# Sums of squares for six residual norms: GpSimd adds seven tiles, TensorE sums two

## The reference

```python
def rms_norm(x, g):
    xf = x.astype(jnp.float32)
    y = xf * lax.rsqrt(jnp.mean(xf * xf, -1, keepdims=True) + NORM_EPS)
    return (y * g.astype(jnp.float32)).astype(x.dtype)

for l in range(DEPTH):                     # first stack
    h = rms_norm(x, attn_norm_g[l])
    ...
    x = x + merged @ w_out[l]
    h2 = rms_norm(x, mlp_norm_g[l])
    x = x + jnp.square(jax.nn.relu(h2 @ mlp_up[l])) @ mlp_down[l]
return rms_norm(x, final_norm_g)
...
for layer in range(DEPTH):                 # second stack
    h = rmsnorm(x, norm_mix[layer]) * (1.0 + sc1) + sh1
    ...                                    # y: a gated delta rule with attention, or latent attention
    x = x + g1 * y
    h = rmsnorm(x, norm_ffn[layer]) * (1.0 + sc2) + sh2
    x = x + g2 * peer_ffn(h, ...)
return rmsnorm(x, final_norm)
```

## Time and profile before

| | |
|---|---|
| median of 3 runs | 3479.36 us (3476.62 to 3481.10) |
| the profiled execution | 3475.42 us |
| its span in the profile | 3473.6 us |
| PE busy | 3393.0 us (98%) |
| DVE busy | 2452.4 us (71%) |
| ACT busy | 1631.6 us (47%) |
| POOL busy | 323.6 us (9%) |
| DMA, mean | 163 GB/s |

### The profile page before, as it was taken

One profiled execution on the slowest core, in us unless ns is written; L12 is line 12 of the kernel. 1 busy time (PEld: TensorE's weight loads), 2 busy tenths in 40 slices (PEclk: granted clock), 3 DMA queues, 4 the chain that ended last, 5 costly groups with the idle time before them and its releaser, 6 DMA issues.

```text
span 3473.6 us, 69683 instructions
## 1 busy us (share of the span) xinstructions
PE 3393.0 (98%) x24714; PEld 3070.1 (88%) x24714; DVE 2452.4 (71%) x5105; ACT 1631.6 (47%) x3275; POOL 323.6 (9%) x438
## 2 busy tenths in 40 slices
PE   8999999999999999999999999999999999999998
PEld 7879899988888998889988888888889888888887
DVE  6734457665434866537998888888538998888887
ACT  5153355433423743235555555555445555555554
POOL 0212000020210000000370000000000550000000
PEclk9999999999999999989999999999999999999999
DMA  8633378864335976234337887777444258787875
GB/s 231 177 90 94 110 220 268 239 178 136 87 93 155 270 233 162 62 88 138 111 101 195 196 196 191 197 195 186 106 132 151 84 135 195 193 194 194 195 195 135
DMA packets 644022, 565.20 MB, mean 163 GB/s; under 512 B 62027, under 2 KB 589402, under 8 KB 643546
## 3 DMA queue, kind: packets, MB, share of 16 engines
q1 hardware_dynamic: 638564, 542.16, 59.1%
q0 software_dynamic: 4960, 19.93, 1.7%
q10 hardware_dynamic: 278, 0.08, 0.0%
HBM read 550.52 MB, written 9.44 MB: 161 GB/s over the span
## 4 chain that ended last, share of the span: by engine, by line
PE 88%; DVE 7%; ACT 2%; issue 1%; DMA 1%; SPq 0%; POOL 0%; DVEq 0%; ACTq 0%; POOLq 0%
PE bank L1461 15%; PE bank L878 15%; PE bank L856 14%; PE bank L1481 7%; PE bank L1475 7%; PE bank L1478 7%; PE bank L899 4%; PE bank L1411 3%; PE bank L1436 2%; PE bank L852 2%; DVE uT L3331 2%; PE bank L1390 1%; PE bank L1270 1%; PE bank L967 1%; PE bank L1421 1%
## 5 line engine op out<-in xcount | busy, mean ns | idle before, releaser
L1461 PE MATMUL bank<-t_high,u_parts 128*128 128x256 f32 x3072 | 424.8, 280 | 1.3 <-ACT u_parts L2200 1.3
L1461 PEld LDWEIGHTS bank<-t_high,u_parts 128*128 128x128 f32 x3072 | 403.2, 188 | 20.9 <-ACT u_parts L2200 3.0
L3370 DVE TENSOR_TENSOR v_low<-ring,v_high 128x512 fp32r<-128x512 f32 x512 | 337.0, 690 | 59.7 <-ACT v_high L2212 35.4
L1481 PE MATMUL bank<-v_low,w_high 128*128 128x512 f32 x1024 | 323.1, 397 | 0.0
L1475 PE MATMUL bank<-v_high,w_high 128*128 128x512 f32 x1024 | 318.8, 392 | 0.9 <-ACT v_high L2212 0.9
L2212 ACT ACTIVATE v_high<-ring 128x512 fp32r<-128x512 f32 x512 | 299.2, 620 | 38.3 <-PE bank L1481 38.2
L1478 PE MATMUL bank<-v_high,w_low 128*128 128x512 f32 x1024 | 316.1, 390 | 0.0
L2415 POOL TENSOR_SCALAR uT<-cst,selT 128x128 f32<-128x128 f32 x256 | 188.2, 744 | 1312.7 <-ACT selT L2137 1308.4
L2200 ACT ACTIVATE u_parts<-bank 128x512 fp32r<-128x512 f32 x384 | 219.9, 594 | 191.3 <-DVE bank L3342 188.3
L1764 ACT ACTIVATE arena<-bank 128x256 f32<-128x256 f32 (+1 forms) x270 | 103.8, 387 | 437.7 <-PE bank L856 242.2
L856 PE MATMUL bank<-hT,ring 128*128 128x256 f32 (+2 forms) x1232 | 277.6, 382 | 8.3 <-DVE hT L2640 6.1
(11 more groups left out here) (467 smaller groups left out, 6423.7 us busy)
## 6 DMA issues: line engine op xcount, KB each, us to landing
ring<-in_peer_v SPq DMA_DIRECT2D x256, 512.0 KB, 4.5
ring<-in_peer_u SPq DMA_DIRECT2D x768, 128.0 KB, 4.3
ring<-in_w_in SPq DMA_DIRECT2D x128, 512.0 KB, 4.1
ring<-in_mlp_up SPq DMA_DIRECT2D x64, 512.0 KB, 4.2
uT<-in_mod_w SPq DMA_DIRECT2D x64, 512.0 KB, 5.1
ring<-in_mlp_down SPq DMA_DIRECT2D x64, 512.0 KB, 4.4
ring<-in_peer_u SPq DMA_DIRECT2D x64, 512.0 KB, 3.8
arena<-in_mod_w POOLq DMA_DIRECT2D x32, 512.0 KB, 4.9
```

Of the source, the lines that this page charges most:

```text
L1461: ins = eng.matmul(PB[6 + b][:, 0:S], u_parts[:, part, k * P:k * P + P], moving[:, k, :], start=(n == 0), stop=(n == len(products) - 1))
L1481: ins = eng.matmul(PB[2 * tt + q][:, :], w_high[:, b, t], v_low[:, j % 4, d], start=False, stop=last)
L3370: tt_(v_low[:, j % 4, d], ring[:, 2 + j % 4, d], v_high[:, d].bitcast(F32), ALU.subtract).then_inc(sem("vL_ready"), 1)
```

## The change

GpSimd gets the sum over the tiles. With each square that ScalarE signals, `squares_added` adds the running sum in place: square[1] = square[0] + square[1], up to square[6], which then holds the sum of tiles 0 to 6, and signals sq_added after each add. Each add waits for the one before. In down of layer 1 there are two adds in each step, first in hT, then in square. TensorE waits for the sixth sq_added, multiplies ones with tile 6, waits for the eighth sq_ready, and multiplies ones with tile 7. Nothing of the square sums is left between the projection's tiles. The other square sums (the first norm, the latent norms, the raw columns of the second stack's layer 1, the final norm) stay as they are.

```diff
-            def square_pair(k):
-
-                if k == 0 and pe.reused("ss_read", 1):
...
+            def residual_sum(k):
+
+                if k < KD - 1:
+                    return
+                if pe.reused("ss_read", 1):
+                    eng.wait_ge(sem("ss_read"), pe.freed("ss_read", 1))
+                eng.wait_ge(sem("sq_added"), pe.next("sq_added", KD - 2))
+                eng.matmul(PB[4][:, 0:S], C("ones"), square[:, KD - 2, :], start=True, stop=False)
+                eng.wait_ge(sem("sq_ready"), pe.next("sq_ready", KD))
+                eng.matmul(PB[4][:, 0:S], C("ones"), square[:, KD - 1, :], start=False, stop=True).then_inc(sem("ss_ready"), 1)
+
+            def residual_pair(k):
...
+                eng.wait_ge(sem("sq_added"), pe.next("sq_added", KD - 2))
+                for bank, sq in ((4, square), (5, hT)):
+                    eng.matmul(PB[bank][:, 0:S], C("ones"), sq[:, KD - 2, :], start=True, stop=False)
+                eng.wait_ge(sem("sq_ready"), pe.next("sq_ready", KD))
+                for bank, sq in ((4, square), (5, hT)):
+                    ins = eng.matmul(PB[bank][:, 0:S], C("ones"), sq[:, KD - 1, :], start=False, stop=True)
+                ins.then_inc(sem("ss_ready"), 1)
...
+            def to_residual(one):
 
                 for m in range(KD):
                     one(m)
-                    if m >= 2:
-                        square_in(m - 2)
-                for m in range(KD - 2, last):
-                    square_in(m)
...
+                to_residual(down)
                 if l == 0:
-                    to_residual(down)
+                    residual_sum(KD - 1)
                 else:
-                    to_residual(down, square_pair, last=0)
-                    raw_tiles([("conv", j) for j in range(RAW)], raw_conv, S + 1, square_pair)
+                    raw_tiles([("conv", j) for j in range(RAW)], raw_conv, S + 1, residual_pair)
...
+            def squares_added(both=False):
+
+                for k in range(KD):
+                    eng.wait_ge(sem("sq_ready"), pool.next("sq_ready"))
+                    if 0 < k < KD - 1:
+                        if k > 1:
+                            eng.wait_ge(sem("sq_added"), pool.seen["sq_added"])
+                        if both:
+                            tt_(hT[:, k, :], hT[:, k - 1, :], hT[:, k, :], ALU.add)
+                        tt_(square[:, k, :], square[:, k - 1, :], square[:, k, :], ALU.add).then_inc(sem("sq_added"), 1)
+                        pool.next("sq_added")
...
                 for b in (0, 3):
                     gated(l, b)
+                squares_added()
+                squares_added(l == 1)
...
             for l in range(DEPTH):
+                if l == 1:
+                    pool.next("sq_ready", KD + 6)
+                squares_added()
                 gate_rows(l)
```

More of the change, by code:

```diff
@@ L929, in norm_sum @@
                     square_sum(square, k, KD, bank)
-            def square_pair(k):
-                if k == 0 and pe.reused("ss_read", 1):
+            def residual_sum(k):
+                if k < KD - 1:
+                    return
+                if pe.reused("ss_read", 1):
                     eng.wait_ge(sem("ss_read"), pe.freed("ss_read", 1))
-                eng.wait_ge(sem("sq_ready"), pe.next("sq_ready"))
-                eng.matmul(PB[4][:, 0:S], C("ones"), square[:, k, :], start=(k == 0), stop=(k == KD - 1))
-                ins = eng.matmul(PB[5][:, 0:S], C("ones"), hT[:, k, :], start=(k == 0), stop=(k == KD - 1))
-                if k == KD - 1:
-                    ins.then_inc(sem("ss_ready"), 1)
-            def to_residual(one, square_in=lambda k: square_sum(square, k, KD), last=KD):
+                eng.wait_ge(sem("sq_added"), pe.next("sq_added", KD - 2))
[3 more added lines that the diff above has]
+            def residual_pair(k):
+                if k < KD - 1:
+                    return
+                if pe.reused("ss_read", 1):
+                    eng.wait_ge(sem("ss_read"), pe.freed("ss_read", 1))
[7 more added lines that the diff above has]
+            def to_residual(one):
                 for m in range(KD):
                     one(m)
-                    if m >= 2:
-                        square_in(m - 2)
-                for m in range(KD - 2, last):
-                    square_in(m)
             raws = [0]
@@ L1670, in _ @@
                 eng.wait_ge(sem("gated_b"), pe.next("gated_b", KD))
-                to_residual(lambda m: stream(("wout", l, m), lambda i: merged[:, i, :]), last=0)
+                to_residual(lambda m: stream(("wout", l, m), lambda i: merged[:, i, :]))
                 norms[0] += 1
-                raw_tiles([("up", l, j) for j in range(RAW)], raw_up, S, lambda k: square_sum(square, k, KD))
+                raw_tiles([("up", l, j) for j in range(RAW)], raw_up, S, residual_sum)
                 for j in range(RAW, DFF // P):
@@ L1724, in mix @@
                         stream(("mix", l, m), lambda i: mix_t[:, i, :])
-                to_residual(mix, last=0)
+                to_residual(mix)
                 norms[0] += 1
-                raw_tiles([("pq", l, j) for j in range(RAW)], raw_pq, S + 1, lambda k: square_sum(square, k, KD))
+                raw_tiles([("pq", l, j) for j in range(RAW)], raw_pq, S + 1, residual_sum)
                 experts(l)
@@ L2416, in gate_rows @@
                     ins.then_inc(sem("pool_rows"), 1)
+            pool.next("sq_ready", KD)
             for l in range(DEPTH):
```

## The result

The changed kernel took 3458.94 us (median of 5 runs, 3454.16 to 3464.89), the kernel before 3477.91 us on the same chip (5 runs, 3473.92 to 3481.1): ratio 0.9946, 95% interval 0.9935 to 0.9957, 19.0 us less. One of the later executions of the kernel before took 12505.4 us at a mean granted clock of 0.407; it counts in no figure here.

A forecast was written before the change was run, and what follows sets the result against it. TensorE, busy 98% of the span, was taken to set the pace. Gains 4.90 + 1.55 + 3.81 + 3.44 = 13.70 us against the 3479.36 us median gave 3465.7 us (chance 0.50), range 3460 to 3474.

The forecast's parts named there:

- mix, both: Mix stages of both layers: 2.15 us ahead of tile 7's end plus 0.30 in the tail, twice: 4.90 us gain.
- down 0: Down, layer 0: 2.15 us gained, less 0.60 because the sum comes later in the tail: 1.55 us gain.
- down 1: Down, layer 1, with two sums: 4.30 us gained, less 0.49 in the tail: 3.81 us gain.
- wout, both: Wout, both layers: the mod_w transfer sets the tail, only four slots of 0.43 us count per layer: 3.44 us gain.
- Rival A: Residual stages: every removed slot comes off, tails hidden or adds shorter: 18.06 us gain, 3461.3 us; chance 0.10.
- What one product costs: TensorE, ones times a tile of squares: one slot of 0.43 us, 42 products removed.
- The add in the tail: GpSimd's last add, after square 6: 0.73 us, with 0.15 us before its start and 0.05 to PE's start.
- 0.59 behind VectorE: Mix tail: GpSimd's add, begun inside VectorE's residual operation, ends 0.59 us after it, the same as unblocked.
- Rival B: Tails cost more: adds of 1.53 us (gain 9.7), mod_w landing unmoved (10.3), or both (6.3, 3473.1 us); chance 0.22.
- Rival C: Behind the stages: the gain is given back at a join that PE doesn't clock, 3479.4 us; chance 0.12.
- Rival E: The change doesn't do what it says: PE's order still has eight products; chance 0.02.
- Rival D: Down stages: GpSimd's add holds VectorE back from weight_low, PE waits: 13.8 us slower, 3493 us; chance 0.04.

The follow-up runs named there:

- e10: The kernel before, unedited, measured against itself: 3475.29 us, ratio 1.0000.
- second and third comparison: The changed kernel, unedited, timed again twice beside the kernel before: 3462.34 us (ratio 0.9962), then 3459.53 us (ratio 0.9953).
- e5: Changed kernel, but in the down stages GpSimd adds only tiles 0 to 5 and TensorE does three products: 3460.85 us, ratio 0.9962 to before.
- e6: Changed kernel with the first mod_w transfer of each first-stack layer issued two ring loads sooner: 3461.95 us, ratio 0.9964 to before.
- e2: Changed kernel without GpSimd's adds, so the sums of tiles 0 to 5 are missing: 3459.21 us, ratio 0.9951 to before.
- e4: Changed kernel with one more GpSimd operation in front of the last add of every residual: 3466.87 us, ratio 0.9975 to before.
- e3: Kernel before with all its products, plus GpSimd's adds, their sums unused; TensorE waits for the last add: 3480.57 us, ratio 1.0016.

## Why the prediction missed

**The sum was right.** Term by term, in us of gain; measured is the first pair of profiles, with the wout terms at equal landing of the mod_w transfer:

| term | forecast | measured |
|---|---|---|
| mix, both | 4.90 | 2.29 + 2.30 = 4.59 |
| down 0 | 1.55 | 1.44 |
| down 1 | 3.81 | 3.86 |
| wout, both | 3.44 | 1.73 + 1.72 = 3.45 |
| sum | 13.70 | 13.34 |

For wout 0 the profiles differ by 1.80, of which 0.07 is the landing (5.45 against 5.38). For wout 1 I set after against e10, 29.76 less 28.04, since the transfer took 5.05 and 5.06 in these two. In the first profile of before it took 6.25. VectorE's first use of it there:

```profile
1109.29 0.58 SPq L2458 DMA_DIRECT2D uT<-in_mod_w  x1
...
1115.54 0.76 DVE L3019 TENSOR_SCALAR arena<-uT,cond 128x1024 f32<-128x1024 f32 x1 [2.10 <-DMA uT<-in_mod_w]
```

So the first pair shows 2.92 in this stage, 1.2 of it not from the change. On average over the profiles such landings add 0.8 to the sum (14.1), and the runs say 14.2 at equal clock and 14.7 in their medians. I can't tell 13.3 from 14.7 by runs that scatter by 3 us.

**The step that failed is the base, and with it the range's low end.** The prediction set its sum of 13.70 against the median of three runs, 3479.36, which gave 3465.7, and not against the profiled execution's 3475.42, which gave 3461.7. All 69 runs of the kernel before put it at 3475.7: the base was 3.7 too high. Then the range took "the scatter of the runs (some 2 us)", where three runs lay within 4.5 us; it is 3.2 to 3.6 us for one run, and a median of five of the changed kernel came out at 3458.9, 3462.3 and 3459.5. The 6.8 us between 3465.7 and 3458.94 are, within rounding, 3.7 of base, 1.0 of gain (14.7 in the medians, 13.7 in the sum) and 2.0 by which the first five runs fell below the long-run median of 3460.9. Rival A's 3461.3 against the high base, less 2, made 3460; against 3475.4 it would have been 3457.4, less the true scatter about 3454, and the measured time would have lain inside.

Two parts of this are luck. That the profiled execution gave a base within 0.3 of the long-run median was one: the changed kernel's first profiled execution, 3464.89, lay 4.0 above its own. And which side of 3460 a median of five falls on was another: 9 of the 15 runs of the changed kernel lie in the range, and so does the median of all.

**Where the other 5 us of the first comparison went.** 19.0 less 14 is not in any stage that the change touches, and the second and third comparison gave 13.3 and 16.2. It is scatter: the five runs of before lay 2.3 above its long-run median, those of the changed kernel 2.0 below its own. The scatter goes with the granted clock. The part of the program that varies most is the gated delta rule ahead of mix, layer 0; e5 took 203.6 us there and e6 197.2 with the same code in this part. Windows of e5 (its part starts at 1302.2):

```profile
1400.00:1450.00 50.00, 46.66 (x635) 43.09 (x634) 23.95 (x62) 9.18 (x24) 0.00 (x0) 0.93 0.22 65
1450.00:1500.00 50.00, 48.12 (x205) 39.38 (x204) 19.50 (x61) 14.12 (x41) 0.00 (x0) 0.62 0.00 1
```

and of e6 (1301.0):

```profile
1400.00:1450.00 50.00, 45.82 (x622) 42.03 (x617) 25.50 (x67) 9.89 (x27) 0.00 (x0) 1.00 0.21 61
1450.00:1500.00 50.00, 48.32 (x212) 40.34 (x212) 19.03 (x59) 13.87 (x41) 0.00 (x0) 0.69 0.02 7
```

PE is busy for 46 to 48 of 50 us in both, at 0.93 and 0.62 in one and at 1.00 and 0.69 in the other. Over the whole part the granted clock was 0.883 in e5, 0.913 in e6 and 0.922 in e10, which took 195.9 us; over all twelve profiles the part's length and its clock have a correlation of -0.93. That the clock and the time go together is measured; what makes the clock differ from run to run was not tried, and stays open.

**Point by point.**
- What one product costs, 0.43 us: right, by e2 to 0.01 in two stages.
- The add in the tail, 0.73 us: right in size and place. The gap from GpSimd's end to PE's start was 0.15 (658.61 to 658.76) and not 0.05, and against it square 6 reached GpSimd in 0.07 and not 0.15. The first product behind the wait kept its slot for 0.51 us and not 0.43 (658.76 to 659.27). In down 0 the statistic came 3.10 behind T where 3.0 was forecast, in down 1 the last pair 3.91 where 3.96.
- Mix: 0.14 of further gain in the tail where 0.30 was forecast (PE's wait 0.22 by the slots, 0.14 forecast). The bound "0.59 behind VectorE" held to 0.01 us and did bind: the add took 0.79 and ended 1.81 behind T, where 1.82 was forecast. What was mis-sized stands behind it: PE started 0.15 behind the add's end and not 0.05, and the two slots took 0.94 (1524.86 to 1525.80) and not 0.86.
- wout: tiles come every 3.45 us (462.11 and 465.56 on ScalarE), the issue moved by four slots, and PE's idle time around the sum is 0.29 + 1.68 = 1.97 by slots (467.04 to 467.33, and 467.76 to 469.44), "about 2". All as forecast.
- Rival A: refuted by e2 (the adds cost 2.6), by e4 (they are on the path), and by wout, where 3.45 us came of the 5.16 of twelve slots.
- Rival B: adds over 1 us exist (1.72 at most, and 1.49 in the median of L2391), but none in a tail. The mod_w transfer landed 1.2 late once, in the kernel before.
- Rival C: refuted. The gain stands in the runs in full. Rival E too: 84 records are gone.
- Rival D: its hold is real and its price is not. GpSimd's add and VectorE's split, in the changed kernel, down, layer 0:

```profile
610.96 0.74 POOL L2392 TENSOR_TENSOR arena<-arena 128x256 f32<-128x256 f32 x1 [10.69 <-ACT arena L1803]
611.07 1.71 DVE L3084 TENSOR_TENSOR weight_low<-ring,weight_high 128x1024 fp32r<-128x1024 f32 x1
```

The split takes 1.71 us in place of 1.22 and ends 1.08 behind the add's end. But it has 3.8 us of lead, and PE's products follow without a gap (610.89, 611.85, 612.81). e3, with all the adds and no product taken off, has no wait of PE for these weights in any of the stages. The point from which this rival decides was judged rightly.

## What to carry to other kernels

Cut a profile at the borders of the stages that a change touches: here that difference repeated to 0.01 us in four of six stages, while whole executions of one kernel scatter by 3 us, so a gain of 0.4% could be read from two profiles and not from three runs. Take a forecast's base from many runs, not from three or from one profiled execution, and size the range by the scatter that many runs show, of the base and of the median that will be measured. Work moved to a slower engine is free only up to its last step: order it so that the last tile or two stay on the fast engine (e5: one more product of 0.43 us in a wait took the add of 0.7 us off the path).

## What the runs showed of the hardware

- The run time of this kernel goes with the mean granted clock of TensorE, 2.0 us for each 0.001, between 0.986 and 0.993; one stage of small products with the same code took 195.9 to 203.6 us, at 0.922 and 0.883. In the six residual stages of the two kernels' five profiles it stayed at 1.00.
- Behind a wait of PE of 2.01 us (e4) the slot of a product was 0.85 in place of 0.43 us and the granted clock was 0.64 in the 4 us from 1308. Behind 1.07 us, at the same place of the changed kernel, the slots stayed at 0.43. In wout of e4, with waits of 1.07 and 0.57 us in both layers, the clock fell to 0.50 for 3 us in layer 1 and not at all in layer 0. A tail's price is thus not always its length: 0.93 us of extra work on GpSimd cost 1.48.
- GpSimd and VectorE hold each other both ways, and the one that is held ends a fixed time behind the other. Adds of 0.73 us became 0.79 in mix, 0.86 in wout and as much as 1.72 in down, layer 1, and each of these ended 0.58 to 0.60 behind VectorE's operation. Splits of 1.22 us became 1.71 to 1.80 and ended 1.08 behind the add. A tensor_scalar of one input went from 0.75 to 1.22 and 1.05 us (e6, e4), ending 0.55 to 0.56 behind the add.
- From GpSimd's end to PE's start it was 0.14 to 0.15 us at all the places above; the earlier trace rows had shown 0.05. The product that PE started then kept its slot for 0.51 us, where the next one took 0.43.
- The mod_w transfer took 4.97 to 6.25 us from issue to first use in one and the same place (wout, layer 1, nine profiles).
